# Attention: the products that spread the softmax divisors, moved past the scores of two units on

## The reference, cut to what matters

```
s = (q @ k.T) * scale           # layer 0: banded mask and a sink; layer 1: all 512 keys; latent: causal
p = exp(s - max(s))
o = (p @ v) / sum(p)            # layer 0 adds exp(sink - max) to the sum
```

## Time and profile before

| | us |
|---|---|
| median of 3 runs | 2143.35 |
| lowest and highest of them | 2140.54, 2145.37 |
| span of the profiled execution (the page gives no other time for it) | 2140.0 |
| PE busy in it | 2012.0 |
| DVE busy | 1117.7 |
| ACT busy | 658.6 |
| attention of layer 0, about | 104 to 196 |
| attention of layer 1, about | 722 to 836 |
| latent attention, about | 1612 to 1671 |

### The profile page before, as it was taken

The page is one execution under the profiler, slowest core; times in us unless marked ns, Lnnn a source line. Parts: engine busy times, 40 slices in busy tenths (PEclk is TensorE's granted clock), DMA queues, the critical chain, the costliest instruction groups (busy, mean ns, idle before and its releaser), DMA issues. The chain is left out here.

```text
span 2140.0 us, 30374 instructions
## 1 busy us (share of the span) xinstructions
PE 2012.0 (94%) x12684; PEld 1474.1 (69%) x12684; DVE 1117.7 (52%) x2039; ACT 658.6 (31%) x1224; POOL 97.7 (5%) x117
## 2 busy tenths in 40 slices
PE   8989999999999989999999999888998999999777
PEld 4766788888865666788888877767656788854333
DVE  5377745446344676745355466556446655532114
ACT  3275323223121465322223234333126422101001
POOL 0000000000000000000000000111000000011102
PEclk9999999999999999999999999999999999999999
DMA  8200246332140300223232241000020134699996
GB/s 292 79 1 1 79 157 233 121 109 88 69 148 0 128 1 1 79 92 105 79 118 79 81 140 65 24 3 3 24 79 21 60 98 163 260 377 423 424 422 249
DMA packets 114827, 266.36 MB, mean 124 GB/s; under 512 B 8931, under 2 KB 71754, under 8 KB 105663
## 3 DMA queue, kind: packets, MB, share of 16 engines
q1 hardware_dynamic: 108638, 250.24, 31.8%
q0 software_dynamic: 5472, 12.02, 1.5%
q10 hardware_dynamic: 576, 2.10, 0.2%
HBM read 258.62 MB, written 26.21 MB: 133 GB/s over the span
## 5 line engine op out<-in xcount | busy, mean ns | idle before, releaser
L236 PE MATMUL ps<-arena 64*64 64x64 f32 (+11 forms) x6484 | 769.3, 332 | 75.7 <-DMA arena<-in_moe_w_gu 19.1
L236 PEld LDWEIGHTS ps<-arena 64*64 64x64 f32 (+3 forms) x6484 | 439.8, 148 | 369.5 <-issue 268.3
L404 DVE TENSOR_SCALAR arena<-arena 128x1024 int32<-128x1024 int32 (+1 forms) x225 | 150.3, 668 | 121.1 <-PE ps L242 83.8
L246 PE MATMUL ps<-arena 128*128 128x128 f32 (+3 forms) x1182 | 159.9, 280 | 34.4 <-DVE arena L926 11.6
L246 PEld LDWEIGHTS ps<-arena 128*128 128x128 f32 (+3 forms) x1182 | 133.0, 149 | 80.3 <-issue 36.0
L240 PE MATMUL ps<-HTr,WH1r 128*128 128x512 f32 (+1 forms) x448 | 169.3, 378 | 2.4 <-ACT WH1r L411 1.2
L240 PE MATMUL ps<-HTr,WH0r 128*128 128x512 f32 (+1 forms) x448 | 169.2, 378 | 1.2 <-ACT T16r L1119 1.2
L411 ACT ACTIVATE WH0r<-arena 128x1024 fp32r<-128x1024 f32 x86 | 91.4, 1063 | 192.1 <-DVE slot2r L407 84.2
L242 PE MATMUL ps<-T16r,WH1r 128*128 128x512 f32 (+1 forms) x384 | 144.0, 375 | 0.0
L242 PE MATMUL ps<-T16r,WH0r 128*128 128x512 f32 (+1 forms) x384 | 144.0, 375 | 0.0
L411 ACT ACTIVATE WH1r<-arena 128x1024 fp32r<-128x1024 f32 x82 | 87.1, 1064 | 181.3 <-DVE slot0r L407 96.7
(11 more groups left out here) (615 smaller groups left out, 3146.7 us busy)
## 6 DMA issues: line engine op xcount, KB each, us to landing
arena<-in_moe_w_gu SPq DMA_DIRECT2D x28, 2048.0 KB, 27.1
arena<-in_w_gate_up SPq DMA_DIRECT2D x44, 1024.0 KB, 7.4
arena<-in_moe_w_down SPq DMA_DIRECT2D x32, 1024.0 KB, 29.3
arena<-in_w_down SPq DMA_DIRECT2D x8, 2048.0 KB, 7.8
arena<-in_w_in SPq DMA_DIRECT2D x7, 2048.0 KB, 8.1
arena<-in_w_in SPq DMA_DIRECT2D x9, 1024.0 KB, 5.5
arena<-in_w_o SPq DMA_DIRECT2D x4, 2048.0 KB, 7.9
arena<-in_moe_w_gu SPq DMA_DIRECT2D x8, 1024.0 KB, 32.6
```

Of the source, the lines that this page charges most:

```text
L236: return e.matmul(o, l, r, start=start, stop=stop, skip_group_check=True)
L246: return e.transpose(o, i, ident[0:n, 0:n])
L404: e.tensor_scalar(h.bitcast(I32), raw.bitcast(I32), -4096, None, ALU.bitwise_and).then_inc(*v_half.up(*name, "mask"))
```

## The change

TensorE asks for the bank of the divisor products of unit u, and issues them, after the scores of u + 2 and just ahead of the values of u; before, it did so straight after the transposes of u. ScalarE's copy to RDEN comes after its part of `made_ready` for u + 2; before, it came ahead of it. Nothing is added or left out, and VectorE's program stays as it is. The order of the bank requests changes with the move. In the last two turns of each call there are no scores of n + 2, and the order there is as before.

```
@@ p_attention
             for n, u in enumerate(us):
                 p_turns(e, u)
-                p_divisors(e, u)
                 if n + 2 < len(us):
                     if l < 2:
                         made_ready(e, l, n + 2, p_prepare, p_mkv_turn)
...
                     p_scores(e, us[n + 2])
+                p_divisors(e, u)
                 p_values(e, u)
@@ a_attention
                 a_turns(e, u, before(names, n, 1 if l == 2 else 2))
-                a_divisors(e, u, before(names, n, 1))
                 if n + 2 < len(us) and l < 2:
                     made_ready(e, l, n + 2, a_prepare, a_mkv_turn)
+                a_divisors(e, u, before(names, n, 1))
                 beside(n)
```

## The result

| | before | after |
|---|---|---|
| median, us | 2143.45 (10 runs, 2140.54 to 2145.63) | 2150.45 (10 runs, 2146.27 to 2151.64) |
| ratio | | 1.0028, 95% interval 1.0019 to 1.0036 |
| span of the profiled execution | 2140.0 | 2147.8 |

The medians lie 7.0 us apart; the ratio makes it 6.0 us, between 4.1 and 7.7. 7.9 us were forecast. The profiled spans lie 7.8 us apart. That the sum comes so near is in part luck: in this profile the layers cost about half of what was written and the latent attention 3 us more than was written, and the stages show it.

A forecast was written before the change was run, and what follows sets the result against it. Taken as bound by TensorE, busiest but waiting for VectorE's splits in preparing turns; 4.6 (layer 1) + 3.5 (layer 0) − 0.3 (last turns) + 0.1 (latent) = 7.9 us on 2143.35 gives 2151.3, range 2146 to 2154.5.

The forecast's parts named there:

- The mechanism: Preparing turns, layers 0 and 1: moved products leave TensorE's wait for VectorE, which grows 0.95 to about 1.5 us; turns lengthen 0.58.
- The price of one set in the new seat: Divisor products between scores and values cost 0.58 us a set, bounds 0.45 and 0.66.
- The products change seats, 0: Layer 1, turns 5 and 9 to 13, which prepare nothing: products swap places with the scores at no cost, 0 us.
- Turns 5 and 9 of layer 0: Their values wait 0.6 us for ScalarE; the 0.58 us delay of turns 4 and 8 falls into that wait.
- The last turns: End of layers 0 and 1: earlier scores of units 14 and 15 gain 0.15 us each layer, 0.3 in all.
- The latent attention: Long waits ahead of the values stay, ScalarE runs 0.1 us late at most: 0.1 us more, bounds 0 and 0.4.
- The lower clock that I gave 0.03 of the chance: Rival, chance 0.03: TensorE's longer waits in a row of turns lower its clock, some 5 us lost, 2156.3 us.
- ScalarE's edit at 0: Copy to RDEN behind the prepared queries costs 0, bounds −0.2 and +0.5; queries and keys are read two turns later or more.
- Absorbed later: Rival, chance 0.12: TensorE's waits for the experts' weights take up to 7.9 us of the delay; 2143.4 to 2147 us.

The follow-up runs named there:

- The doubled products: Each divisor-product set in preparing turns of layers 0 and 1 issued twice: on the kernel before 2144.1 us, ratio 1.0002; on the changed kernel 2156.86 us, ratio 1.0061.
- latent only: Against the kernel before: products moved late only in the latent attention, layers 0 and 1 and ScalarE as before; 2144.47 us, ratio 1.0008.
- the wait filled: The changed kernel plus eight unread TensorE products ahead of the values in turn 2 of each latent group; 2148.2 us, ratio 1.0021 to the kernel before.
- TensorE only: Against the kernel before: products moved late except in turns 0 and 4 of layers 0 and 1, ScalarE's copy unmoved; 2147.7 us, ratio 1.0019.
- doubled in the new seat: The changed kernel with each divisor-product set in preparing turns of layers 0 and 1 issued twice; 2156.86 us, ratio 1.0061 to the kernel before.
- layers only: The changed kernel with products left early in the latent attention, ScalarE's edit in; 2147.05 us, ratio 1.0018 to the kernel before.
- the change again: The whole change against the kernel before, run once more for more times and a second profile; 2150.54 us in 5 runs, ratio 1.0036.

## Why the prediction was right, and where it was not

The forecast of the total held, and so did the mechanism in the preparing turns. But the price of a set was put too high, the turns that prepare nothing were put at 0 where they gain, and the latent attention was put at 0.1 where both profiles of the change have 3 us. The first two errors lie one way and the third the other; how near the total came is luck.

*The mechanism* was right, step by step. The products were hidden in TensorE's wait for VectorE, the wait grew to 1.53 us (1.5 was written), the preparation stayed 3.5 us after the transposes, and the next turn gave nothing back. The doubled products show it in both directions.

*The price of one set in the new seat* is the term of the sum that was mis-sized: 0.43 to 0.46 us, not 0.58. I took the distance from products to the scores behind them, and this seems to contain a change from one kind of matmul group to another. Between scores and values that change is there anyway (products and values are both 128*64, the scores 128*128), so only the eight matmuls themselves are added. The rows fit this (a second set behind the first costs 0.44 us in either seat), but no run changes the kind of a group alone. The lower bound of 0.45, given for just this reason, was the value. 16 sets at 0.44 are 7.0 us; the turns below take back 1.5 in layer 1 and 1.3 in layer 0, which leaves 4.1 or 4.2.

*"The products change seats, 0"* failed. In the turns that prepare nothing the old seat costs 0.76 and the new one 0.44 us. In layer 1 turns 5 and 9 to 14 became 1.5 us shorter, in layer 0 turns 10 to 14 0.4; without turn 14 (see the last turns, below) 1.3 and 0.2. The rows for it stood in the same timeline; I had compared the order and not the neighbours.

*Turns 5 and 9 of layer 0* were right: their wait for L855 shrank and they came out 0.44 us shorter each, by the whole delay of the turn before them. With the products doubled they took back that delay too. TensorE in turn 9 after, which answers to the earlier trace rows:

```profile
175.00 1.51 PE L236 MATMUL ps<-arena 128*64 128x256 f32 x12 [0.37 <-ACT arena L855]
```

*The last turns* were right in kind: the wait ahead of the values of unit 14 fell by 0.27 us in layer 1, and turn 14, whose own order is unchanged, is 0.28 us shorter in layer 0 and 0.27 in layer 1. That is 0.55 us for both layers, where 0.3 was written. The wait of unit 14 in the kernel after:

```profile
836.26 1.11 PE L236 MATMUL ps<-arena 128*64 128x128 f32 x16 [0.72 <-ACT arena L855]
```

So the two layers cost 4.1 us, where the sum had 7.8: 16 sets at 0.44 us, less 0.9 in turns 5 and 9 of layer 0, 1.5 in the other turns that prepare nothing, and 0.55 in the last ones.

*The latent attention* was right as a pipeline: three profiles with the new order at full clock have the stage at 16.0 and 29.95 us (latent only, the wait filled, TensorE only). It was wrong by the clock: 3.0 us in the profiled execution, not 0.1. The lower clock that I gave 0.03 of the chance came, but not in the layers' waits of 1.5 us, which I had in mind, in that profile. The evidence over all profiles is a tendency and no rule. With the change's order in the latent stage the clock fell there in three of five (the change twice, doubled in the new seat; not in latent only, TensorE only), with the short waits of before or the filled one in one of seven. In layers 0 and 1 it fell in three of six profiles that have the waits of 1.5 us (layers only, the wait filled, doubled in the new seat) and in none of six that have the old ones. All four of these falls stand in turns with several preparations: once in turn 0 of layer 0, behind waits of 1.91 and 0.25 us, and three times in turn 4, behind one of 1.53 or 1.60 us and one of 0.25 or 0.26. None stands in a turn whose only such wait is 1.53 us, and TensorE only, which keeps the old seat in turns 0 and 4, had none. Over the runs, the time at the lower level can be estimated as twice the distance of a run's granted clock from 1, times its span: the ten of the kernel after had a mean of 39.5 us, 33 of before 37.3. If half of these 2.2 us is lost, that is 1.1 us of the 7. The rest of the runs don't agree on it: the five of the change again had 41.3 us against 36.9 of the 21 of before that go with them, layers only 34.8 and latent only 37.4. So neither part alone has clearly more than before, and the size stays open. Of the profiled 3.0 us in the latent stage most seems to be chance of that execution, though it came out much the same (3.2) in the second profile.

The Trainium skill (TensorE: Matmul & The Clock Gate, A second HAM failure mode: psum-queue depth-cycling) says that short idle times between groups make the clock swing. I had put it aside for the waits of these stages. The runs go some way towards it: swings came more often with the longer waits. But by it alone latent only should have swung, and did not.

*ScalarE's edit at 0.* In the whole change that holds by the waits: no matmul's wait names its copy. (Six weight loads in layer 0 do, each behind an idle time of 0.38 or 0.39 us, as weight loads at this place have it in the kernel before too, and the matmuls behind them have no wait.) But the reasons were incomplete. "These are read two turns later" left out that the bank of the prepared queries must be emptied before TensorE can ask for it again: 0.26 us, twice in layer 0, when the copy stands behind late products. And alone the edit makes the layers 1.9 us longer, 1.0 of it in waits that name it, of 3.1 measured.

*Absorbed later.* TensorE's waits for the experts' weights are 18.9 us where they were 20.9 (19.1 and 1.8), and the rest of the program is 1.0 us shorter. In the twelve profiles this piece varies between 467.6 and 470.8 us, by no order that follows the delay, and latent only, with no delay in the layers, has 17.6 us of these waits. So nothing of this rival is shown. The queue's waits for TensorE grew from 1280.1 to 1287.3 us, by about the delay.

*What stays open.* The layers' 4.1 us are shown. With some 1.1 us for the clock it is 5.2, between the ends of the ratio's interval (4.1 to 7.7 us) and 1.8 under the 7.0 of the medians. Whether the clock's part is real, and where the 1.8 us are if they are not noise, no run here can tell.

## What to carry to other kernels

Work that sits inside a wait for another engine is free there and costs its length wherever its engine has nothing to wait for; before such work is moved, look at which turns have the wait, and consider moving it in the others alone. Doubling the work in its place is a cheap test: if the time stays and the wait shrinks by what was added, it is hidden. A sum can be near the total while its stages are wrong, so check each stage against its own term. The price of a group of matmuls depends on its neighbours, so read it from the same neighbours as in the new place (start to start of the whole row of groups, with and without it), not from its own distance to the next one.

## What the runs showed of the hardware

- Eight matmuls of 128*64 on 128x128 cost 0.76 us between transposes and scores and 0.44 us ahead of the values of the same form. A second set behind the first cost 0.44 us too.
- The clock fell behind a wait of 1.87 us in one execution (3.22 us for 24 matmuls) and held behind waits of 2.20 us in two others (1.92): the length of the one wait ahead doesn't decide it. While it was low in layer 1 of the kernel with doubled products, the scores took 3.02 us instead of 2.09:

```profile
779.98 3.02 PE L236 MATMUL ps<-KST,QST 128*128 128x512 f32 x8
787.40 2.09 PE L236 MATMUL ps<-KST,QST 128*128 128x512 f32 x8
```
